# A two-layer decoder step: projection halves beside the top-k ranking and the sample's turned rows, the attention's tail in another order, and waits by tile ahead of the output and down projections

## The reference

```
h = rms_norm(x, g_mix)
q, k, v, qi, ki, wi, qr, fr, ir, gr, ga, gb = split_columns(h @ w_in)
# (A) attention, 8 heads of 64 over 4 KV heads, on the keys that an indexer ranks highest
sc = sum_h wi[t,h] * relu(qi[t,h] . ki[s]);  idx = top_k(sc);  att = softmax(q k[idx]) v[idx]
# (B) gated linear recurrence, 4 heads, key and value dimension 128, in chunks of 64
S_t = diag(f_t) S_{t-1} + (1 - f_t) i_t^T;   o_t = S_t^T q_t
rec = rms_norm(o, g_rec) * silu(gr)
x = x + (sigmoid(ga) * (att @ w_pa) + sigmoid(gb) * (rec @ w_pb)) @ w_o
h = rms_norm(x, norm_ffn);  x = x + (silu(h @ w_gate) * (h @ w_up)) @ w_down      # hidden 2816
```

## Time and profile before

| | us |
|---|---|
| median of three runs | 2236.66 (2236.39, 2236.66, 2238.34) |
| the profiled execution, its own time | 2234.92 |
| span of the profiled execution | 2233.1 |
| PE busy in it | 2043.2 (91%) |
| DVE, ACT, POOL busy | 1199.4, 787.5, 761.4 |
| mean granted TensorE clock, share of full speed | 0.945 |

### The profile page before, as it was taken

The page is one execution under the profiler, slowest core; times in us unless marked ns, Lnnn a source line. Parts: engine busy times, 40 slices in busy tenths (PEclk is TensorE's granted clock), DMA queues, the critical chain, the costliest instruction groups (busy, mean ns, idle before and its releaser), DMA issues. The chain is left out here.

```text
span 2233.1 us, 40190 instructions
## 1 busy us (share of the span) xinstructions
PE 2043.2 (91%) x15630; PEld 1936.6 (87%) x15630; DVE 1199.4 (54%) x2159; ACT 787.5 (35%) x1215; POOL 761.4 (34%) x414
## 2 busy tenths in 40 slices
PE   3998899887898999999999899998888899999998
PEld 2987799866698999999999889996767899999998
DVE  3387677666455543045346786885654564412533
ACT  3243222366233432222323342234642343322223
POOL 0642248200034433434355223650001443334433
PEclk9999999878799999999999999997897999999999
DMA  5312236101332232332241322531033322223322
GB/s 128 107 58 76 58 101 178 57 27 44 113 89 85 85 91 65 98 94 74 72 147 51 95 58 72 153 116 41 1 97 96 99 85 86 83 74 100 89 63 79
DMA packets 309368, 189.08 MB, mean 85 GB/s; under 512 B 15904, under 2 KB 295552, under 8 KB 308224
## 3 DMA queue, kind: packets, MB, share of 16 engines
q1 hardware_dynamic: 299616, 160.51, 25.3%
q0 software_dynamic: 4224, 16.78, 2.2%
q10 hardware_dynamic: 5408, 10.16, 1.3%
HBM read 167.47 MB, written 18.10 MB: 83 GB/s over the span
## 5 line engine op out<-in xcount | busy, mean ns | idle before, releaser
L655 POOL TENSOR_TENSOR w_lo<-raw,w_hi 128x1024 fp32r<-128x1024 f32 (+3 forms) x290 | 630.4, 2175 | 1349.5 <-ACT w_hi L1391 1349.1
L797 PE MATMUL acc<-normed,w_hi 128*128 128x268 f32 x5696 | 961.8, 291 | 18.3 <-POOL w_lo L655 16.9
L797 PEld LDWEIGHTS acc<-normed,w_hi 128*128 128x128 f32 x5696 | 806.8, 191 | 41.4 <-issue 21.0
L1391 ACT ACTIVATE w_hi<-raw 128x1024 fp32r<-128x1024 f32 (+1 forms) x290 | 293.5, 1013 | 976.3 <-PE acc L797 976.3
L797 PE MATMUL acc<-normed,w_lo 128*128 128x268 f32 x2848 | 587.8, 288 | 0.0
L797 PEld LDWEIGHTS acc<-normed,w_lo 128*128 128x128 f32 x2848 | 448.7, 190 | 0.0
L797 PE MATMUL acc<-hidden,w_hi 128*128 128x268 f32 x1408 | 237.8, 292 | 15.6 <-DVE hidden L2488 15.6
L797 PEld LDWEIGHTS acc<-hidden,w_hi 128*128 128x128 f32 x1408 | 202.7, 194 | 16.4 <-issue 16.4
L797 PE MATMUL acc<-hidden,w_lo 128*128 128x268 f32 x704 | 146.5, 290 | 0.0
L2488 DVE TENSOR_TENSOR hidden<-act_f,hidden 128x536 f32 x44 | 92.8, 2109 | 51.2 <-ACT hidden L1735 51.2
L2481 DVE TENSOR_TENSOR silu<-silu,rnorm 128x536 f32<-128x536 f32 x44 | 83.5, 1898 | 59.3 <-ACT silu L1732 59.3
(11 more groups left out here) (327 smaller groups left out, 2876.2 us busy)
## 6 DMA issues: line engine op xcount, KB each, us to landing
raw<-in_w_in_dram SPq DMA_DIRECT2D x90, 512.0 KB
raw<-in_w_gu_dram SPq DMA_DIRECT2D x88, 512.0 KB
raw<-in_w_down_dram SPq DMA_DIRECT2D x32, 384.0 KB
raw<-in_w_down_dram SPq DMA_DIRECT2D x32, 320.0 KB
gate_scratch<-gate_out ACTq DMA_DIRECT2D x32, 268.0 KB
normed<-gate_scratch SPq DMA_DIRECT2D x4, 2144.0 KB, 8.1
raw<-in_w_o_dram SPq DMA_DIRECT2D x16, 512.0 KB
raw<-in_w_pa_dram SPq DMA_DIRECT2D x16, 256.0 KB
```

The source lines that it names most:

```text
L655: pool.tensor_tensor(w_lo[s][:, 0:kt, :], raw[slot][:, 0:kt, :], w_hi[s][:, 0:kt, :].bitcast(f32), ALU.subtract).then_inc(lo_done, 1)
L797: mm = pe.matmul(acc[o][:, half, 0:HT], w[s][:, k, :], mov[:, part, k0 + k, half * HT:(half + 1) * HT], start=start and n == 0, stop=stop ...
L1391: act.activation(w_hi[slot % 2][:, 0:kt, :], raw[slot][:, 0:kt, :], ACT.Copy).then_inc(hi_done, 1)
```

## The change

In every layer:

- **Ranking.** Unit UB+8 stood whole behind `starts`; now its k 0 to 4 stand ahead of `ties`, its k 4 to 8 between `ties` and `starts`.
- **Sample's rows.** `sel_rows` (L760 at the gates' unit 19) stands between the two K halves of unit 19 and no longer behind it. On DVE the partial output of gate unit 23 (`next_part`) comes ahead of `sel_swap`.
- **Start of the attention.** PE's waits for `sel_swap` and `v_turn` 2 move from ahead of qk(0) to behind qk(1); `v_sample` and `k_sample` (8 transposes) move from behind turn(0) to ahead of it. ACT gets a one-element Exp ahead of its wait for the gates' spill.
- **Block 3.** Its turn becomes ten 128x128 transposes, the fifth of each half into acc; the picking of 16 in 32 columns moves into ACT's copies, pT gets a dense layout, `level_tail` 7 moves from ahead of pv(3) to behind it.
- **Tail.** ACT's att_hi moves to its step 17, DVE's att_lo to its step 17, `sample_state` 2 and `v_blk` 3 to step 18. PE interleaves att units 0 to 3 with `rec_sample` 2, `rank1` 3 (now in work[1]) and `rec_sample` 3; `rec_sums` comes behind att unit 3, the spreads behind att unit 4. The squares 2 and 3 go to `tmp`, so that the first two need not be used up first. SP's and POOL's lists stay the same.
- **Output projection.** Units 0 and 1 run k 0 to 6 once six tiles of `merged` are there, and k 6 to 8 once all eight are.
- **Down projections.** The first K half waits for the first 6 (5) hidden tiles of the part, the second for all.
- A count of the DVE-side order (`_STEPS`) goes from 8 to 9.

The diff, cut to its core:

```diff
-                  19: [("state", 4), ("sample_state", 2), ("v_blk", 3), ("sample_state", 3)]}
+                  18: [("state", 3), ("sample_state", 2), ("v_blk", 3)], 19: [("state", 4)]}
...
+        def squared(h):
+            return sq[:, h, :] if h < 2 else tmp[:, h - 2, :]
+        def rank_tile(h, half):
+            return work[1][:, 512 * half:512 * half + 512] if h == 3 else acc[half][:, 1, :]
...
+                unit_part(UB + 8, 0, 0, 4, KT, normed, 0, 0, OB // 2 + 4)
                 ps = begin("ties")
                 wait(pe, "mask_counts", L, 3, 2)
...
+                unit_part(UB + 8, 0, 4, KT, KT, normed, 0, 0, OB // 2 + 4)
...
-                    unit(UB + 8 + n, n % 2, KT, normed, 0, n % 2, OB // 2 + 4 + n // 2)
+                    if n == 19:
+                        unit_part(UB + 8 + n, n % 2, 0, 4, KT, normed, 0, n % 2, OB // 2 + 4 + n // 2)
+                        sel_rows()
+                        unit_part(UB + 8 + n, n % 2, 4, KT, KT, normed, 0, n % 2, OB // 2 + 4 + n // 2)
+                    elif n:
+                        unit(UB + 8 + n, n % 2, KT, normed, 0, n % 2, OB // 2 + 4 + n // 2)
                     for step in BEHIND.get(n, ()):
...
-                        if j == 4:
-                            mm = pe.matmul(ps[0:w, c * 64:c * 64 + 64], E[:, s, c * P:c * P + w],
-                                           ident.rearrange("p (m t) -> p m t", t=32)[:, :, 0:16], start=True, stop=True)
-                        else:
-                            mm = transpose(ps[0:w, c * n:c * n + n], E[0:n, s, c * P:c * P + w])
+                        at = ps[0:w, c * P:c * P + P] if c < 4 else last_turn(s)
+                        mm = transpose(at, E[:, s, c * P:c * P + w])
                     mm.then_inc(turn_filled[s], 1)
...
+                    if h == 3:
+                        wait_rec_drained(pe, L, ("rec_out", 4))
+                        wait_rec_drained(pe, L, ("state", 4))
...
-                        pe.matmul(rank_tile(half), k_s[:, h * P:(h + 1) * P], v_blk[:, half * 4:half * 4 + 4, :],
+                        pe.matmul(rank_tile(h, half), k_s[:, h * P:(h + 1) * P], v_blk[:, half * 4:half * 4 + 4, :],
...
-                wait_drained(pe, L, "sel_swap")
-                wait_drained(pe, L, ("v_turn", 2))
...
+                    if block == 0:
+                        wait_drained(pe, L, "sel_swap")
+                        wait_drained(pe, L, ("v_turn", 2))
+                        hold(pe)
+                        rec_steps(["v_sample", "k_sample"])
...
-                for name in (("state", 4), ("rec_out", 4)):
-                    wait_rec_drained(pe, L, name)
...
-                wait(pe, "sample_drained", L, 4, 4)
+                wait(pe, "s0_ready", L, 32, 24)
...
                 att_unit(0)
+                late_sample(2)
+                att_unit(1)
+                rank1(3)
+                att_unit(2)
+                late_sample(3)
+                att_unit(3)
+                wait(pe, "sample_drained", L, 4, 4)
+                hold(pe)
                 ps = begin("rec_sums")
...
-                                       sq[:, h % 2, half * HT:(half + 1) * HT], start=True, stop=True)
-                    if h < 2:
-                        mm.then_inc(S["rec_squares_used"], 1)
+                                       squared(h)[:, half * HT:(half + 1) * HT], start=True, stop=True)
                 finish(mm, "rec_sums")
-                att_unit(1)
-                att_unit(2)
+                att_unit(4)
...
-                for n in range(3, KT):
+                for n in range(5, KT):
                     att_unit(n)
...
-                wait(pe, "merged_hi", L, 8, 8)
-                wait(pe, "merged_lo", L, 8, 8)
-                hold(pe)
-                with pe.Fori(0, 4) as g:
+                for k_at, k_end in ((0, 6), (6, KT)):
+                    wait(pe, "merged_hi", L, 8, k_end)
+                    wait(pe, "merged_lo", L, 8, k_end)
+                    hold(pe)
+                    for i in range(2):
+                        unit_part(UO + i, i, k_at, k_end, KT, merged, 0, i, OO // 2)
...
-                    wait(pe, "hid_lo", L, 22, 12 if part == 0 else 22)
-                    wait(pe, "hid_hi", L, 22, 12 if part == 0 else 22)
-                    hold(pe)
-                    with pe.Fori(0, 4) as g:
+                    for i in range(4):
+                        if i < 2:
+                            ready = 12 * part + kt * (i + 1)
+                            wait(pe, "hid_lo", L, 22, ready)
+                            wait(pe, "hid_hi", L, 22, ready)
+                            hold(pe)
+                        unit(UD[part] + i, i % 2, kt, hidden, kt * (i % 2), i // 2, OD[part] // 2,
+                             start=i % 2 == 0, stop=i % 2 == 1)
...
+                so(act.activation(row_st[:, 0, 1:2], eps[:, 0:1], ACT.Exp))
...
+                def att_high():
+                    wait(act, "pv_drained", L, BLOCKS, BLOCKS)
+                    wait(act, "att_ready", L, 4, 4)
+                    act.wait_ge(S["tok_stored"], L * 144 + 144)
...
+                            so(act.activation(short_turned(s)[:, 0:256].rearrange("p (m t) -> p m t", t=16),
+                                              ps.rearrange("p (m t) -> p m t", t=32)[:, :, 0:16], ACT.Copy))
+                            act.activation(short_turned(s)[0:16, 256:320].rearrange("p (m t) -> p m t", t=16),
+                                           last_turn(s).rearrange("p (m t) -> p m t", t=32)[:, :, 0:16],
+                                           ACT.Copy).then_inc(turn_drained[s], 1)
...
+                split_merge(2)
+                sample_drain(2)
+                split_merge(3)
+                wait(act, "sample_drained", L, 4, 2)
                 wait_rec_drained(act, L, ("rec_out", 4))
                 wait_rec_drained(act, L, ("rec_out", 3))
...
-                for h in range(4):
-                    rec_square(h)
-                split_merge(2)
+                rec_square(0)
+                rec_square(1)
+                split_merge(4)
+                sample_drain(3)
+                wait(act, "sample_drained", L, 4, 4)
+                rec_square(2)
+                rec_square(3)
+                split_merge(5)
...
-                split_merge(3)
-                split_merge(4)
+                split_merge(6)
...
+                    if n - 1 == 22:
+                        next_part()
                     if n - 1 in (18, 19, 20, 21, 22):
                         (sel_rows, sel_weights, sel_probs, sel_pv, sel_swap)[n - 19]()
-                    next_part()
+                    if n - 1 != 22:
+                        next_part()
...
+                att_merge(0)
+                sample_state(3)
+                att_merge(1)
+                att_merge(2)
+                wait(vec, "sample_drained", L, 4, 4)
...
-_STEPS = (173, 8)
+_STEPS = (173, 9)
```

More of the change, by code:

```diff
@@ L155, in build @@
                 12: [("level", 5, 0), ("level_tail", 5)], 13: [("level", 6, 0), ("level_tail", 6)]}
[L156 removed]
+    PE_AMID = {3: [("v_turn", 3), ("v_turn", 4)], 4: [("level", 0, 1)],
                6: [("level", 1, 1)], 7: [("level", 2, 1)], 9: [("level", 3, 1)], 10: [("level", 4, 1)],
@@ L428, in turn_tile_of, with last_turn, short_turned @@
             return work[0][:, 512 * s:512 * s + 512]
+        def last_turn(s):
+            return acc[s][0:16, 1, 0:128]
+        def short_turned(s):
+            return pT[:, s, :, :].rearrange("p c t -> p (c t)")
         def pv_tile():
@@ L1639, in rec_steps @@
                             query_exp()
+                        elif step == "att_hi":
+                            att_high()
                         else:
                             rec_drain((v_s if step == "v_sample" else k_s)[:, :], step, lambda ps: ps[0:NB, :])
+                def att_high():
+                    wait(act, "pv_drained", L, BLOCKS, BLOCKS)
+                    wait(act, "att_ready", L, 4, 4)
+                    act.wait_ge(S["tok_stored"], L * 144 + 144)
+                    hold(act)
+                    for n in range(4):
+                        act.activation(att_hl[:, 0, n, :], A[:, n, :], ACT.Copy).then_inc(S["att_hi"], 1)
                 def att_exps(block):
@@ L1705, in _ @@
                     act.activation(rec_hl[:, 0, h, :], B[:, 8 + h, :], ACT.Copy).then_inc(S["rec_hi"], 1)
-                for n in range(5, 8):
-                    split_merge(n)
+                split_merge(7)
                 split_merge(8)
@@ L2361, in sample_state, with att_low @@
                                 ps[:, m * P:(m + 1) * P], ALU.mult, ALU.add).then_inc(S["s0_ready"], 1)
+                def att_low():
+                    for n in range(4):
+                        wait(vec, "att_hi", L, 4, n + 1)
+                        TT(att_hl[:, 1, n, :], A[:, n, :], att_hl[:, 0, n, :].bitcast(f32), ALU.subtract)\
```

(9 more changed lines are left out.)

59 lines of the change are left out of this document (26 added, 33 removed).

## The result

The changed kernel takes 2179.78 us (2177.8 to 2186.08, four runs) against 2237.5 (2236.39 to 2239.6): ratio 0.9753, 95% interval 0.9739 to 0.9767. The forecast was 2173, its range 2156 to 2190.

What follows compares the result with a forecast made beforehand. PE was taken as the bound, busy 2043.2 of 2233.1 us. Terms summed to 31.8 a layer, 63.6 in two; 2234.92 minus that is 2171.3, and with 1.7 for the median 2173, range 2156 to 2190.

Steps and rivals of the forecast that it cites:

- Ranking: PE's gaps up to ties and starts: a unit split in halves gains 5.9 us a layer, 4.4 to 6.
- Sample's rows and attention's start: From PE's gap at sel_rows to behind turn(0): moved work and waits gain 5.1 us a layer, 3 to 6.5.
- the sign: Attention's start in the changed profile: turn(0) about 10 us earlier than 450.58 (5.9 + 1.2 + 2.8).
- the 3.9 of turn(0) and the transposes: Attention's start: turn(0) 2.8 us earlier (1.4 to 3.4), and 1.1 of the 8 transposes in idle time (0 to 1.9).
- the three: Slack at sel_rows 1.2, earlier turn(0) 2.8, transposes 1.1: together 5.1 us a layer, low end 3, high end 6.5.
- Block 3: Block 3's turn: ten transposes for twenty matmuls, 2.2 instead of 4.19 us, gain 2.0 a layer, 1 to 2.
- Tail: Interleaved att units fill PE's gaps, but UP+4's load queues behind the gate return: gain 2 us a layer, -3 to +8.
- Output projection: Start on six merged tiles: PE starts 4.2 us earlier, 1.1 more from the clock, gain 5.3 a layer, 4 to 6.5.
- Two units of 36 matmuls are 8.9 at full clock: Output projection: the last two merged tiles are in by the time these first parts, 8.9 us, are done.
- Down projections: Waits by hidden tile remove gaps of 4.0 and 3.7 and half-clock losses: gain 11.5 us a layer, 8 to 12.
- The rival of giving back: Attention's start gains 1.5, ranking 4.4, tail -1, through DVE and the clock: 8.1 less a layer, 2189 us; chance .22.

Runs made afterwards that it cites:

- experiments 9 and 10: Changed kernel with sel_rows as before in both; first also output unit 0 alone in parts and UP+4 to UP+7 loads earlier, 2141.68; second also ranking as before, 2186.58.
- experiment 1: Changed kernel with block 3's turn, pT layout and level_tail 7 as before: 2195.34 us, ratio 0.9818.
- Experiment 3: Changed kernel with SP's loads of UP+4 to UP+7 ahead of the last state store and gate return: 2157.29 us, ratio 0.9653.
- experiment 2: Changed kernel with only unit 0 of the output projection in two parts, unit 1 whole: 2172.54 us, ratio 0.9718.
- experiment 7: Kernel before the change with the down projections' waits by tile alone: 2214.92 us against 2234.31, ratio 0.991.
- experiment 12: Changed kernel measured again without any edit: 2178.84 us, ratio 0.9739.

## Why the prediction was right, and where it was not

Faster was right, and 57.7 of 63.6 us came. By its own terms:

- **Ranking**: 5.9 forecast, 6.3 read; experiments 9 and 10, apart up to there in the ranking alone, are 6.5 apart at qk(0), and the whole is slower without it.
- **Sample's rows and attention's start**: this step failed, 5.1 forecast against -2.3. The prediction took `sel_rows` to move half a unit up, and the section on the change says that it stood behind unit 19; it stood ahead of unit 19, and moves half a unit down. That DVE is what is late, and that a gap comes back ahead of `sel_probs`, was right; that it comes back bigger, with POOL's w_lo holding DVE (0.22 became 2.19) and a low clock (0.68) in a stretch where PE has no slack, was not seen. Turn(0) came at 447.72, 2.9 earlier than the earlier trace rows where about 10 was named as the sign. For the start itself the trace has 3.4, 1.5 ahead of qk(0) and 1.9 behind it, for the 3.9 of turn(0) and the transposes. The low end given for the three was 3, and no bound reached below nothing.
- **Block 3**: 2.0 forecast, 8 by experiment 1, about 5 of them in the block. The term counted matmuls and priced them by rows at a low clock; it left out that the clock over the whole block, with pv's 80 matmuls, would change.
- **Tail**: the mechanism (queue, split, drain, squares) and its sizes were right: 7.2 of wait for 6.5, 1.63 for 1.5, and 2.8 for 2 in all. Experiment 3 takes the 7.2 away; no run takes back the interleaving itself, so the 2.8 are read from the rows alone.
- **Output projection**: 5.3 forecast, 1.4 read. The start was right: 2.50 is left of 6.9, so 4.4 earlier for 4.2. The step that failed is "Two units of 36 matmuls are 8.9 at full clock": it asked whether the last tiles are in by then and not when the units' buffers come free. With one unit in parts (experiment 2) the 5.3 come.
- **Down projections**: 11.5 forecast, 12.1 read, and experiment 7 agrees (12.1 by its rows, 8 to 12 by its interval).
- The rival of giving back named the attention's start and the ranking; the giving back lay in the sample's rows and the output projection instead. That the sum came out near is also luck: block 3's 6 too few, and 1.6 more in the other blocks, stand against 7.4 and 3.9 too many, and the 1.6 are not there in the first layer of experiment 12.

## What to carry to other kernels

Before a wait is covered by splitting work, ask which buffer the split work holds open and what its release triggers; one unit in parts covered most of the wait, two made a new one of 2.25. A load that a later stage needs belongs ahead of a bulk transfer in the same queue. Where a gap lies matters, and not only how long it is: 3.04 with a low clock behind it cost little where DVE was late anyway, 3.89 in a stretch without slack cost more than the move had to gain. Nor does every gap bring the low clock: in experiment 3 the clock was 1.00 behind 2.53 and 2.26.

## What the runs showed of the hardware

- DVE's 64x8 instruction took 0.22 alone, and 2.19 and 2.18 in two forms beside a POOL tensor instruction, ending with it within 0.03 us; a 64x1 TENSOR_TENSOR took 0.15 alone and 1.22 in the same way; MAX8 and MATCH_REPLACE8 took their usual 0.66 to 0.68 beside POOL's w_lo of 415.84 to 418.19.
- Ten transposes with a dense pT in place of twenty 64-column matmuls raised the granted clock over block 3 from 0.51 to 0.82 (0.56 with the old form in the changed kernel), though PE was busy nearly all of the window in each.
- Gaps of PE of 2.50 and 2.25 us in the output projection had clocks of 0.66 and 0.67 behind them in one kernel, and gaps of 2.53 and 2.26 at the same places a clock of 1.00 in another (experiment 3).
